# The step size dt leaves the decay exponent: masked C·B products are multiplied by it on GpSimd

## The chip, the cores and the metric

One core of a Trainium2 chip runs the whole program. The metric is the device time of one execution in microseconds (us), the median of several runs. "The profile" and "the trace" are one profiled execution of the same program. The engines are TensorE (PE, matrix products; PEld are its weight loads), VectorE (DVE), ScalarE (ACT), GpSimd (POOL) and SyncE (SP, which here only starts DMAs). Each runs its own instructions in order and waits for the others on semaphores.

## The reference

One layer over 512 latent tokens with a context prefix of 256 tokens, D = 1024, all in f32. It has a token mixer (a bidirectional Mamba-2 scan of 16 heads in 4 groups, beside a gated short convolution, one input and one output projection) and then a PEER mixer, which for every token picks 16 experts in each of 8 heads and gathers their rows. The part that this case is about is the scan inside a chunk of 128 tokens:

```python
xdt = xs * dt[..., None]                      # per token and head
acs = jnp.cumsum(a, axis=2)                   # a = dt * A, log decay
seg = acs[:, :, :, None] - acs[:, :, None, :]
decay = jnp.exp(jnp.where(lower, seg, -jnp.inf))
cb = jnp.einsum('bclgn,bcsgn->bclsg', cm, bm)
y_diag = jnp.einsum('bclsg,bclsgr,bcsgrp->bclgrp', cb, decay, xdt)
...
y_f, h_f = ssd_direction(xs, bm, cm, dt[:, :, 0], a[:, :, 0], h0_fwd, False)
y_b, h_b = ssd_direction(xs, bm, cm, dt[:, :, 1], a[:, :, 1], h0_bwd, True)
return y_f + y_b, h_f, h_b
...
y = y + d_skip * xs
```

So each pair (s, l) of tokens of a chunk has a forward factor for s <= l and a backward one for s >= l; on the diagonal both count, with decay 1 and their two step sizes dt.

## The kernel before

The 512 tokens are four tiles of 128 (m = 0 to 3), the context two more. The program has these stages, in order: set-up and the input projection for x, B and C (up to about 205 us); z, transposes and cumulated decays (to 250 us); the state-space stage (250 to 391 us), which also carries the projections of the short convolution for the first half of the tokens; the output projection, normalisation and first queries of tile 0 and in part 1 (to 465 us); and the gather, in which GpSimd starts 512 indirect DMAs of expert rows while VectorE and TensorE use them, and the second half of the mixer's work is threaded in between.

The order of the state-space stage is written out by hand in the list SCHED, and each engine walks this list and issues its own part of every entry. There are ten `step` entries (chunk states, forward and backward in turn) with the `x` entries that prepare their inputs. Then for each tile m and each group g there are `r` (select decays), `m` (the product `mdec` of decays and C·B), `y` (TensorE's diagonal product), `diag` after each second group, `off` and `out` (the part of the states that enter the chunk) and `cb` (C·B of the next tile, placed at the end of the tile before). `proj` entries, 24 in all, stand between them. This text calls a pair (m, g) block b = 4m + g.

For one block: ScalarE starts the load of two rows of cumulated decays for each of four heads, spread over all partitions, into one of three buffers `drows`, two blocks ahead (`load_rows`; it waits until `mdec` of the block before has been formed). `log_decays` (L1280, eight ACTIVATE) adds a bias per partition, `adec`, which is ln(dt) minus the cumulated decay of the row token, for both directions. VectorE's `select_decays` (L1790) picks forward or backward by a triangular mask. ScalarE takes the exponential (L1312). VectorE's `decay_matrix` (L1804) multiplies by C·B into one of three buffers `mdec`. TensorE's `diagonal` (L936) multiplies by `xs`. The selection keeps only one direction on the diagonal; the other one's share, dt times the diagonal of C·B, is added to the skip factor.

C·B itself: TensorE fills a bank (L923), ScalarE copies it to SBUF (L1304, two buffers `cbm`), and VectorE's `c_times_b` (L1777 to L1782) takes out the diagonal by a product with the identity and a sum, and makes `skip`, which `diagonal_part` (L1813) multiplies by `xs`; L1815 adds the bank of the diagonal products. `output` is L1824 (bank times decay), L1827 (add) twice per direction and L1830 (times z). The state update `step` is L1746 and L1748 for each half. L1758, L1759, L1619 are the short convolution's input product and taps, L1765 its gate. L1843 scales groups of y.

On ScalarE the squares of y (`group_squares`, L1242) of tile m − 1 stand behind block (m, 3). On GpSimd this stage has only `squares` of the short convolution (L706, L710, L713), eight times; it walks SCHED for them and holds them back until three `r` entries have gone by. ScalarE's `sc_scale` waits for them two channels later. GpSimd's earlier work, the modulation (L687 to L694), ends at 212 us.

Of the kernel before, what the change touches and what calls it, by code (L numbers as in the profile page):

```python
# [15 lines left out]
ALU = mybir.AluOpType  # L16
ACT = mybir.ActivationFunctionType
AX = mybir.AxisListType.X

P = 128  # L20
# [9 lines left out]
def build(nc, x, x_t, ctx_in, ctx_t, rows_a, rows_b, w_ada, w_in, w_dt, conv_w, dt_bias, a_log, d_skip, w_out, w_q, keys,  # L30
# [311 lines left out]
    with ExitStack() as stack:  # L342
# [3 lines left out]
        def sem(name):  # L346
            return stack.enter_context(nc.semaphore(name))
# [40 lines left out]
        mdec = [at(k, HPG * P) for k in (52, 54, 98)]  # L388
        NMD = len(mdec)
# [52 lines left out]
        cbm = [at(k, NG, P) for k in (128, 130)]  # L442
        cbd, skip = at(135, NG), at(135.25, 2, HEADS)
        cbi = at(132, NG, P)
# [29 lines left out]
        s_cbm, s_ln = sem("cb_products_copied"), sem("steps_logged")  # L474
# [182 lines left out]
        def _(pool):  # L657
# [56 lines left out]

            waiting, n_r = [], 0
            for kind, n in SCHED:
                if kind == "r":
                    n_r += 1
                    if waiting and n_r >= waiting[0][1] + 3:
                        squares(waiting.pop(0)[0])  # L720
                elif kind == "proj" and projs[n][0] == "gb":
                    waiting.append((projs[n][1], n_r))
# [41 lines left out]
        def _(pe):  # L764
# [162 lines left out]
            def diagonal(mg):  # L927
                m, g = mg
                b = m * NG + g
                name = ("y", m, g // 2)  # L930
                yps = claim(name) if g % 2 == 0 else bank_of(name)
                pe.wait_ge(s_m, b + 1)
                for r in range(HPG):
                    h = g * HPG + r
                    col = (h % 8) * HD
                    last = mm(yps[:, col:col + HD], mdec[b % NMD][:, r * P:(r + 1) * P],  # L936
                              xs[:, m, h * HD:(h + 1) * HD], start=True, stop=True)
# [205 lines left out]
        def _(act):  # L1143
# [69 lines left out]
            A(dtl, dts[:], ACT.Ln).then_inc(s_ln, 1)  # L1213
# [74 lines left out]
            for kind, n in SCHED:  # L1288
# [11 lines left out]
                elif kind == "cb":  # L1300
                    ps = await_bank(act, ("cb", n))
                    if n >= 2:
                        act.wait_ge(s_m, (n - 1) * NG)
                    ins = A(cbm[n % 2].rearrange("p g l -> p (g l)"), ps[:, :], ACT.Copy)  # L1304
                    release(ins, ("cb", n))
                    await_read(act, ("cb", n))
                    act.sem_inc(s_cbm, 1)
                elif kind == "r":
# [12 lines left out]
                    if g == NG - 1 and 1 <= m <= NA:  # L1321
                        group_squares(m - 1)
# [215 lines left out]
        def _(dve):  # L1538
# [170 lines left out]
            V.sem_inc(s_acs, 1)  # L1709
            dve.wait_ge(s_edec, 3)  # L1710
# [64 lines left out]
            def c_times_b(m):  # L1775
                dve.wait_ge(s_cbm, m + 1)
                link(V.tensor_tensor(cbi, cbm[m % 2], ident[:].unsqueeze(1).to_broadcast([P, NG, P]), ALU.mult))  # L1777
                link(V.tensor_reduce(out=cbd, in_=cbi, axis=mybir.AxisListType.X, op=ALU.add))
                s = skip[:, m % 2].rearrange("p (g r) -> p g r", r=HPG)
                link(V.tensor_tensor(s, dts[:, 0, m, :].rearrange("p (g r) -> p g r", r=HPG),  # L1780
                                     cbd.unsqueeze(2).to_broadcast([P, NG, HPG]), ALU.mult))
                link(V.tensor_tensor(skip[:, m % 2], skip[:, m % 2], drow[:], ALU.add))  # L1782
# [10 lines left out]
            def decay_matrix(mg):  # L1793
                m, g = mg
                b = m * NG + g
                if b >= NMD:
                    f = b - NMD
                    if f % 2:
                        await_filled(dve, ("y", f // NG, (f % NG) // 2))
                    else:  # L1800
                        dve.wait_ge(s_mu, f // 2 + 1)
                dve.wait_ge(s_cbm, m + 1)
                dve.wait_ge(s_dexp, b + 1)
                V.tensor_tensor(mdec[b % NMD].rearrange("p (r l) -> p r l", l=P),  # L1804
                                cbm[m % 2][:, g].unsqueeze(1).to_broadcast([P, HPG, P]),
                                drows[b % NDR][:, 0].rearrange("p (r l) -> p r l", l=P), ALU.mult).then_inc(s_m, 1)

            def diagonal_part(mh):

                m, h = mh  # L1810
                cols = slice(h * 512, (h + 1) * 512)
                y = yacc[m][:, cols]
                link(V.tensor_tensor(heads(y), heads(xs[:, m, cols]), per_head(skip[:, m % 2, 8 * h:8 * h + 8], 8), ALU.mult))  # L1813
                ps = await_bank(dve, ("y", m, h))
                read_link(V.tensor_tensor(y, y, ps[:, :], ALU.add), ("y", m, h))  # L1815
# [48 lines left out]
            for kind, n in SCHED:  # L1864
# [332 lines left out]
```

## Time and profile before

| what | value |
|---|---|
| median of 3 runs (lowest to highest) | 1859.75 us (1859.25 to 1860.06) |
| the profiled execution's own time | 1860.06 us |
| its span in the trace | 1858.2 us |
| busy: PE, DVE, ACT, POOL | 76%, 77%, 30%, 46% |
| DMA, mean over the span | 356 GB/s |
| 286 to 390 us: PE, DVE, ACT, POOL busy | 94.4, 80.2, 57.5, 11.3 us of 104 |

Times in the trace count from the start of the span. Busy time of an engine doesn't contain its waits, but a VectorE or GpSimd instruction that is held up after it started is shown longer. "L1804" is line 1804 of the kernel. A matmul in f32 shows as two instructions. "Idle before" is the time in which the engine had nothing running just before the named group, and behind the arrow is what ended it.

### The profile page before, as it was taken

To read this page: it belongs to the slowest core of one execution; us is meant where nothing else is said; L and a number is where in the kernel's file an instruction comes from. 1 tells how busy PE (TensorE), PEld (TensorE's weight loads), DVE (VectorE), ACT (ScalarE), POOL (GpSimd) and SP (SyncE) were. 2 spreads that over 40 slices of the span, in tenths; PEclk is the share of its full clock that TensorE was granted. 3 is DMA by queue.
4 is the path that set the end of the run, shared out by engine and by line. 5 is a ranking of instruction groups with operands and counts; after the bars stand their busy time and mean duration, and the time that the engine had idled before them with its cause. 6 is when DMAs were issued, how large, how long until landed. Compare 5 with 4: busy or idle time off the path is not lost.

```text
span 1858.2 us, 15417 instructions
## 1 busy us (share of the span) xinstructions
PE 1404.9 (76%) x4381; PEld 810.2 (44%) x4381; DVE 1439.6 (77%) x2790; ACT 552.4 (30%) x1566; POOL 861.9 (46%) x622
## 2 busy tenths in 40 slices
PE   7999999999688878877878777687655555565554
PEld 2555687888355545544545244343311111111111
DVE  1555468655878779889877988798989889888877
ACT  3110234622332343223313432233322223222222
POOL 0788500011545444444434465456555555555561
PEclk9999999999899999898998799788877787877777
DMA  9543325564999999999999999999999999999996
GB/s 380 193 157 136 137 92 158 165 267 178 386 411 421 421 421 421 421 421 421 420 421 421 370 416 421 422 422 421 422 421 421 422 421 422 421 421 421 422 422 249
DMA packets 95723, 660.96 MB, mean 356 GB/s; under 512 B 10766, under 2 KB 11286, under 8 KB 17302
## 3 DMA queue, kind: packets, MB, share of 16 engines
q0 software_dynamic: 76448, 555.78, 72.6%
q1 hardware_dynamic: 13808, 93.39, 12.8%
q10 hardware_dynamic: 5383, 10.80, 1.9%
q8 instruction: 36, 0.59, 0.1%
q14 instruction: 48, 0.39, 0.1%
HBM read 657.76 MB, written 2.18 MB: 355 GB/s over the span
## 4 chain that ended last, share of the span: by engine, by line
DMA 44%; PE 23%; DVE 20%; issue 6%; ACT 4%; POOL 1%; SPq 0%; DVEq 0%; ACTq 0%; POOLq 0%
DMA arena<-in_peer_uv,arena 42%; PE bank L826 10%; DVE arena L2053 7%; PE bank L1111 5%; DVE arena L2089 4%; PE bank L999 3%; DMA arena<-in_w_ada 2%; PE bank L851 1%; POOL arena L758 1%; DMA arena<-acs_scratch 1%; ACT arena L1472 1%; DVE arena L2016 1%; ACT arena L1280 1%; DVE arena L1746 1%; DVE arena L1748 1%
## 5 line engine op out<-in xcount | busy, mean ns | idle before, releaser
L758 POOL DMA_INDIRECT arena<-in_peer_uv,arena x512 | 707.8, 1382 | 721.6 <-DVE arena L2089 446.3
L1111 PE MATMUL bank<-arena,smalls 128*128 128x512 f32 x1036 | 663.0, 775 | 415.9 <-ACT smalls L1480 415.7
L2053 DVE CUSTOM_DVE_ANT_0 arena<-arena 128x1024 f32<-128x1024 f32 x512 | 619.4, 1223 | 153.3 <-DMA arena<-in_peer_uv,arena 151.8
L1111 PEld LDWEIGHTS bank<-arena,smalls 128*128 128x128 f32 x1036 | 220.2, 231 | 783.5 <-ACT smalls L1480 588.9
L2089 DVE SCALAR_TENSOR_TENSOR arena<-arena 128x1024 f32<-128x1024 f32 x247 | 315.8, 1278 | 37.4 <-ACT arena L1472 34.8
L826 PE MATMUL bank<-arena 128*128 128x256 f32 (+1 forms) x1216 | 329.0, 428 | 1.8 <-ACT arena L1176 1.5
L1467 ACT ACTIVATE arena<-arena 128x2 f32<-128x2 f32 x255 | 51.9, 203 | 925.1 <-DVE arena L2053 925.0
L826 PEld LDWEIGHTS bank<-arena 128*128 128x128 f32 x1216 | 232.7, 192 | 100.9 <-issue 76.1
L1472 ACT ACTIVATE arena<-arena 128x1 f32<-128x1 f32 x510 | 122.5, 287 | 8.5
L1054 PE MATMUL bank<-arena 128*128 128x256 f32 x480 | 108.9, 380 | 0.0
L1480 ACT ACTIVATE smalls<-ident,arena 128x128 f32<-128x128 f32 x259 | 103.6, 401 | 8.3
L1054 PEld LDWEIGHTS bank<-arena 128*128 128x128 f32 x480 | 91.2, 191 | 23.0 <-issue 12.0
L1641 DVE TENSOR_SCALAR arena<-bank,early 128x512 f32<-128x512 f32 (+1 forms) x28 | 18.4, 692 | 67.3 <-PE bank L826 67.3
L687 POOL TENSOR_TENSOR arena<-arena,cs 128x2048 f32<-128x2048 f32 x16 | 57.7, 3606 | 22.3 <-DVE arena L1629 13.5
L1619 DVE SCALAR_TENSOR_TENSOR arena<-bank,early,arena 128x496 f32<-128x496 f32 (+1 forms) x112 | 62.6, 622 | 0.6
L1032 PE MATMUL bank<-arena 128*128 128x256 f32 x256 | 59.6, 387 | 0.0
L851 PE MATMUL bank<-arena 128*128 128x256 f32 x256 | 58.1, 384 | 0.0
L1032 PEld LDWEIGHTS bank<-arena 128*128 128x128 f32 x256 | 50.2, 197 | 15.5 <-issue 9.3
L999 PE MATMUL bank<-arena 128*128 128x256 f32 x256 | 56.0, 379 | 0.0
L851 PEld LDWEIGHTS bank<-arena 128*128 128x128 f32 x256 | 49.4, 194 | 10.7 <-issue 4.4
L710 POOL TENSOR_TENSOR arena<-arena 128x256 f32<-128x256 f32 x7 | 5.4, 775 | 104.3 <-DVE arena L1765 104.3
L999 PEld LDWEIGHTS bank<-arena 128*128 128x128 f32 x256 | 48.4, 190 | 6.5
(282 smaller groups left out, 1216.3 us busy)
## 6 DMA issues: line engine op xcount, KB each, us to landing
arena<-in_w_in SPq DMA_DIRECT2D x40, 1024.0 KB, 8.3
arena<-in_w_ada POOLq DMA_DIRECT2D x16, 1024.0 KB, 5.1
arena<-in_w_out SPq DMA_DIRECT2D x16, 1024.0 KB, 9.4
arena<-in_peer_w_q SPq DMA_DIRECT2D x16, 1024.0 KB, 9.1
arena<-in_w_ada SPq DMA_DIRECT2D x8, 1024.0 KB, 12.9
arena<-acs_scratch ACTq DMA_DIRECT2D x16, 512.0 KB, 4.7
arena<-in_peer_uv,arena POOLq DMA_INDIRECT x512, 19.6
arena<-in_x SPq DMA_DIRECT2D x4, 512.0 KB, 12.2
```

Source lines behind the costliest of these rows:

```text
L758: nc.gpsimd.indirect_dma_start(gslot[slot], None, uv_tab[0], bass.IndirectOffsetOnAxis(eid[t % 2][:, k:k + 1], 0)).then_inc(s_gsl[slot], 16)
L826: last = mm(dst, w[:, k, j * P:(j + 1) * P], hT(k), start=(k == 0), stop=(k == KD - 1))
L851: last = mm(ps[:, i * WCOL:(i + 1) * WCOL], hT_tile(halves[half][i], k), w[:, k, :], start=(k == 0), stop=(k == KD - 1))
L999: last = mm(ps[:, i * WCOL:(i + 1) * WCOL], src, w[:, k, :], start=(k == 0), stop=(k == KD - 1))
L1032: last = mm(ps[:, i * WCOL:(i + 1) * WCOL], src, w[:, k, :], start=(k == 0), stop=(k == KD - 1))
L1054: last = mm(ps[:, i * WCOL:(i + 1) * WCOL], h2T[:, m % NA, k, :], w[:, k, :], start=(k == 0), stop=(k == KD - 1))
L1111: last = mm(acc[h][:, :], diag[:, k % NDG], row_v(n)[:, h * 512:(h + 1) * 512], start=first, stop=last_one)
L1472: A(wexp[:, k + i:k + i + 1], gate[t % 2][:, k + i:k + i + 1], ACT.Copy, scale=gelu[:, k + i:k + i + 1]).then_inc(s_wexp, 1)
L1480: A(diag[:, r % NDG], ident[:], ACT.Copy, scale=wexp[:, k + i:k + i + 1]).then_inc(s_diag, 1)
L1619: return V.scalar_tensor_tensor(out=d, in0=s, scalar=w, in1=d, op0=ALU.mult, op1=ALU.add)
L2053: V.tensor_tensor_reduce(row_u(n), row_u(n), h2[t], 1.0, 0.0, ALU.mult, ALU.add, dots[:, k:k + 1]).then_inc(s_dot, 1)
L2089: V.scalar_tensor_tensor(out=vacc, in0=row_v(n), scalar=w, in1=vacc, op0=ALU.mult, op1=ALU.add).then_inc(s_vadd, 1)
```

## The change

- The logarithm of dt on ScalarE and the operation that forms `adec` from it go. `adec` is now minus the cumulated decay, made earlier, right behind the cumulated sums.
- ScalarE's copy of C·B goes. VectorE reads the bank and writes C·B times the upper and times the lower triangle mask into SBUF (`cbm[:, 0]` and `cbm[:, 1]`, one buffer for the tile), both with the diagonal. `skip` goes, and `diagonal_part` uses the plain skip factor `drow`.
- GpSimd gets `dt_times_cb` at each `r`: two products with dt per head, one for each direction, and their sum, into one of two buffers `mdec`. For this it waits until the diagonal product of two blocks before has been done, and at g = 0 for the masked products.
- VectorE's `decay_matrix` waits for GpSimd and multiplies `mdec` by the decays in place.
- ScalarE's squares of y move from g = 3 to g = 1.

```diff
-        mdec = [at(k, HPG * P) for k in (52, 54, 98)]
-        NMD = len(mdec)
+        mdec = at(52, 2, HPG * P)
+        mback = at(96, 2, HPG * P)
...
+            def dt_times_cb(mg):
+
+                m, g = mg
+                b = m * NG + g
+                if b == 0:
+                    await_filled(pool, ("st", len(steps) - 2, 1))
+                if b >= 2:
+                    f = b - 2
+                    if f % 2:
+                        await_filled(pool, ("y", f // NG, (f % NG) // 2))
+                    else:
+                        pool.wait_ge(s_mu, f // 2 + 1)
+                if g == 0:
+                    pool.wait_ge(s_cbm, m + 1)
+                hs = slice(g * HPG, (g + 1) * HPG)
+                dst = [v[:, b % 2].rearrange("p (r l) -> p r l", l=P) for v in (mdec, mback)]
+                for d in range(2):
+                    nc.gpsimd.tensor_tensor(dst[d], cbm[:, d, g].unsqueeze(1).to_broadcast([P, HPG, P]),
+                                            dts[:, d, m, hs].unsqueeze(2).to_broadcast([P, HPG, P]),
+                                            ALU.mult).then_inc(s_dtcb, 1)
+                pool.wait_ge(s_dtcb, 3 * b + 2)
+                nc.gpsimd.tensor_tensor(mdec[:, b % 2], mdec[:, b % 2], mback[:, b % 2], ALU.add).then_inc(s_dtcb, 1)
...
                 if kind == "r":
+                    dt_times_cb(n)
...
-            A(dtl, dts[:], ACT.Ln).then_inc(s_ln, 1)
...
-                elif kind == "cb":
-                    ps = await_bank(act, ("cb", n))
-                    if n >= 2:
-                        act.wait_ge(s_m, (n - 1) * NG)
-                    ins = A(cbm[n % 2].rearrange("p g l -> p (g l)"), ps[:, :], ACT.Copy)
-                    release(ins, ("cb", n))
-                    await_read(act, ("cb", n))
-                    act.sem_inc(s_cbm, 1)
...
-                    if g == NG - 1 and 1 <= m <= NA:
+                    if g == 1 and 1 <= m <= NA:
                         group_squares(m - 1)
...
+            V.tensor_scalar(adec[:], acs[:], -1.0, None, ALU.mult).then_inc(s_neg, 1)
...
             def c_times_b(m):
-                dve.wait_ge(s_cbm, m + 1)
-                link(V.tensor_tensor(cbi, cbm[m % 2], ident[:].unsqueeze(1).to_broadcast([P, NG, P]), ALU.mult))
-                link(V.tensor_reduce(out=cbd, in_=cbi, axis=mybir.AxisListType.X, op=ALU.add))
...
+                cb = await_bank(dve, ("cb", m)).rearrange("p (g l) -> p g l", g=NG)
+                tri_g = lambda tri: tri[:].unsqueeze(1).to_broadcast([P, NG, P])
+                post(V.tensor_tensor(cbm[:, 0], cb, tri_g(upper), ALU.mult))
+                read_link(V.tensor_tensor(cbm[:, 1], cb, tri_g(lower), ALU.mult), ("cb", m))
+                V.sem_inc(s_cbm, 1)
...
-                dve.wait_ge(s_cbm, m + 1)
+                dve.wait_ge(s_dtcb, 3 * (b + 1))
                 dve.wait_ge(s_dexp, b + 1)
-                V.tensor_tensor(mdec[b % NMD].rearrange("p (r l) -> p r l", l=P),
-                                cbm[m % 2][:, g].unsqueeze(1).to_broadcast([P, HPG, P]),
-                                drows[b % NDR][:, 0].rearrange("p (r l) -> p r l", l=P), ALU.mult).then_inc(s_m, 1)
+                V.tensor_tensor(mdec[:, b % 2], mdec[:, b % 2], drows[b % NDR][:, 0], ALU.mult).then_inc(s_m, 1)
...
-                elif kind == "step" and n == 0:
-                    dve.wait_ge(s_ln, 1)
-                    V.tensor_tensor(adec[:], dtl, acs[:], ALU.subtract).then_inc(s_neg, 1)
-                    step(0)
```

## Rows read from the trace of the kernel before

**Rows 1.** The page, span in 40 slices: busy tenths of the DMA engines.
```profile
DMA  9543325564999999999999999999999999999996
```

**Rows 2.** Stretches of 20 us: busy time of each engine, granted TensorE clock, DMA.
```profile
280.00:300.00 20.00, 15.47 (x70) 12.61 (x69) 17.28 (x29) 8.43 (x22) 1.67 (x2) 0.91 0.50 155
300.00:320.00 20.00, 20.00 (x109) 17.86 (x108) 16.84 (x29) 10.47 (x30) 1.72 (x2) 1.00 0.47 135
```

**Rows 3.** Groups by line, 250 to 392 us: busy, mean ns | idle before, releaser.
```profile
L936 PE MATMUL bank<-arena 128*128 128x64 f32 x128 | 16.9, 275 | 9.6 <-DVE arena L1804 9.5
L1790 DVE COPY_PREDICATED arena<-early,arena 128x512 f32<-128x512 uint32 x16 | 11.8, 740 | 8.7 <-ACT arena L1280 8.4
L1804 DVE TENSOR_TENSOR arena<-arena 128x512 f32<-128x512 f32 x16 | 11.3, 706 | 4.6 <-ACT arena L1312 4.3
L1815 DVE TENSOR_TENSOR arena<-arena,bank 128x512 f32<-128x512 f32 x8 | 5.5, 687 | 0.6 <-PE bank L936 0.3
L1304 ACT ACTIVATE arena<-bank 128x512 f32<-128x512 f32 x4 | 2.3, 587 | 9.1 <-PE bank L923 9.1
```

**Rows 4.** The chain that ended last, 320 to 350 us: start, us, what.
```profile
324.25 8.82 DMA arena<-acs_scratch
```

**Rows 5.** Timeline of TensorE, 290 to 395 us: start, us, what [idle before].
```profile
290.00 1.09 PE L936 MATMUL bank<-arena 128*128 128x64 f32 x8 [2.50 <-DVE arena L1804]
290.92 5.36 PE L826 MATMUL bank<-arena 128*128 128x256 f32 x16
297.90 1.10 PE L936 MATMUL bank<-arena 128*128 128x64 f32 x8 [1.62 <-DVE arena L1804]
298.84 3.67 PE L826 MATMUL bank<-arena 128*128 128x256 f32 x16
...
389.30 1.10 PE L936 MATMUL bank<-arena 128*128 128x64 f32 x8
...
394.57 13.98 PE L999 MATMUL bank<-arena 128*128 128x256 f32 x64
```

**Rows 6.** Three lines of GpSimd's modulation: ns min/median/max, first and last start.
```profile
L687 POOL TENSOR_TENSOR arena<-arena,cs x16: 3592/3614/3617, 53.1 to 204.2; 128x2048 f32<-128x2048 f32 x16
...
L690 POOL TENSOR_TENSOR arena<-arena x16: 2341/2348/2357, 56.8 to 207.9; 128x1024 f32<-128x1024 f32 x16
...
L692 POOL TENSOR_TENSOR arena<-arena x16: 1261/1267/1275, 59.2 to 210.3; 128x512 f32<-128x512 f32 x16
```

**Rows 7.** Timeline of all engines, 272.2 to 274.4 and 324.2 to 327.
```profile
272.30 1.22 DVE L1726 TENSOR_TENSOR arena<-arena,smalls 128x1024 f32<-128x1024 f32 x1
272.46 1.53 POOL L706 TENSOR_TENSOR arena<-arena 128x256 f32<-128x256 f32 x1 [60.09 <-DVE arena L1765]
273.44 1.10 DVE L1746 TENSOR_TENSOR arena<-arena,smalls 128x512 f32<-128x512 f32 x1
...
325.00 0.74 DVE L1804 TENSOR_TENSOR arena<-arena 128x512 f32<-128x512 f32 x1 [0.50 <-ACT arena L1312]
325.27 1.05 POOL L713 TENSOR_TENSOR arena<-arena 128x256 f32<-128x256 f32 x1
325.67 1.21 DVE L1813 TENSOR_TENSOR arena<-arena 128x512 f32<-128x512 f32 x1
```

**Rows 8.** Timeline of VectorE, 286 to 369 us.
```profile
286.67 0.73 DVE L1790 COPY_PREDICATED arena<-early,arena 128x512 f32<-128x512 uint32 x1
...
309.54 0.69 DVE L1777 TENSOR_TENSOR arena<-arena,ident 128x512 f32<-128x512 f32 x1 [0.90 <-ACTq L1307]
...
311.41 0.73 DVE L1790 COPY_PREDICATED arena<-early,arena 128x512 f32<-128x512 uint32 x1
...
319.68 0.74 DVE L1790 COPY_PREDICATED arena<-early,arena 128x512 f32<-128x512 uint32 x1
...
337.76 0.69 DVE L1777 TENSOR_TENSOR arena<-arena,ident 128x512 f32<-128x512 f32 x1 [2.20 <-ACTq L1307]
...
366.67 0.69 DVE L1777 TENSOR_TENSOR arena<-arena,ident 128x512 f32<-128x512 f32 x1 [4.02 <-ACTq L1307]
```

More of the change, by code:

```diff
@@ L441, in build @@
         yacc = [at(160, D)] * NA + [yB[:, m] for m in range(NA)]
-        cbm = [at(k, NG, P) for k in (128, 130)]
-        cbd, skip = at(135, NG), at(135.25, 2, HEADS)
-        cbi = at(132, NG, P)
+        cbm = at(128, 2, NG, P)
         iota_j, iota_i = sb("iota_j", [P, TOP]), sb("iota_i", [P, TOP], mybir.dt.int32)
@@ L473, in build @@
         s_neg, s_ldec = sem("decay_sums_negated"), sem("log_decays_formed")
-        s_cbm, s_ln = sem("cb_products_copied"), sem("steps_logged")
+        s_cbm, s_dtcb = sem("masked_products_ready"), sem("dt_times_products_step")
         s_ldsel, s_dexp = sem("log_decays_selected"), sem("decays_formed")
@@ L935, in diagonal @@
                     col = (h % 8) * HD
-                    last = mm(yps[:, col:col + HD], mdec[b % NMD][:, r * P:(r + 1) * P],
+                    last = mm(yps[:, col:col + HD], mdec[:, b % 2, r * P:(r + 1) * P],
                               xs[:, m, h * HD:(h + 1) * HD], start=True, stop=True)
@@ L1775, in c_times_b @@
             def c_times_b(m):
-                dve.wait_ge(s_cbm, m + 1)
-                link(V.tensor_tensor(cbi, cbm[m % 2], ident[:].unsqueeze(1).to_broadcast([P, NG, P]), ALU.mult))
-                link(V.tensor_reduce(out=cbd, in_=cbi, axis=mybir.AxisListType.X, op=ALU.add))
[L1779 to L1782, printed above, removed]
+                cb = await_bank(dve, ("cb", m)).rearrange("p (g l) -> p g l", g=NG)
[3 more added lines that the diff above has]
+                V.sem_inc(s_cbm, 1)
             def select_decays(mg):
@@ L1795, in decay_matrix @@
                 b = m * NG + g
[L1796 to L1801, printed above, removed]
-                dve.wait_ge(s_cbm, m + 1)
+                dve.wait_ge(s_dtcb, 3 * (b + 1))
                 dve.wait_ge(s_dexp, b + 1)
-                V.tensor_tensor(mdec[b % NMD].rearrange("p (r l) -> p r l", l=P),
-                                cbm[m % 2][:, g].unsqueeze(1).to_broadcast([P, HPG, P]),
-                                drows[b % NDR][:, 0].rearrange("p (r l) -> p r l", l=P), ALU.mult).then_inc(s_m, 1)
+                V.tensor_tensor(mdec[:, b % 2], mdec[:, b % 2], drows[b % NDR][:, 0], ALU.mult).then_inc(s_m, 1)
             def diagonal_part(mh):
@@ L1812, in diagonal_part @@
                 y = yacc[m][:, cols]
-                link(V.tensor_tensor(heads(y), heads(xs[:, m, cols]), per_head(skip[:, m % 2, 8 * h:8 * h + 8], 8), ALU.mult))
+                link(V.tensor_tensor(heads(y), heads(xs[:, m, cols]), per_head(drow[:, 8 * h:8 * h + 8], 8), ALU.mult))
                 ps = await_bank(dve, ("y", m, h))
```

## The prediction

> **What bounds the kernel now.** I read the page first, then stretches, groups and single instructions of the one stage that the diff touches. The DMA line of the page [rows 1] shows two halves: up to slice 10 the DMA engines are partly idle, from about 465 us on they are at 9 tenths in every slice but the last. That second half is the gather of expert rows. Nothing in the diff enters it, so what the first half gains or loses moves the end by about the same amount. The diff lies at 250 to 391 us, in the state-space stage, whose last diagonal product is on TensorE at 389.30 and whose output weights follow at 394.57 [rows 5].
>
> Call the 16 pairs (tile m, group g) blocks b = 4m + g. TensorE can't start a block's diagonal product before VectorE has written `mdec` (L1804). The groups of 250 to 392 us [rows 3] show TensorE idle 9.6 us in front of those products, 9.5 of it for L1804, which is all that its 94.4 busy us leave free of the 104 from 286 to 390. So the stage is bound by two engines in turn: TensorE's own work, plus 9.6 us in which VectorE is late. VectorE is late at b = 0 and 1 (products at 290.00 and 297.90, idle 2.50 and 1.62 before them [rows 5]), and again from b = 9 on. At 324.25 the chain of work passes through the load of a block's decay rows, 8.82 us [rows 4]. At the start of each tile VectorE waits for ScalarE's copy of the C·B product: 0.90, 2.20 and 4.02 us for m = 1, 2, 3 [rows 8].
>
> **The change part by part.**
>
> *ScalarE.* The four copies of C·B (0.587 us each, L1304 [rows 3]) go, and so does the logarithm of dt. VectorE can read the bank as soon as TensorE has filled it. The move of the four squares from g = 3 to g = 1 takes them from in front of that copy. Its new place costs nothing: they stand where ScalarE waits for the next selection.
>
> *VectorE, C·B.* The product with the identity, the reduction and two small operations, 1.87 us with their gaps from 309.54 to 311.41 [rows 8], are replaced by two mask products that read a bank. The nearest row is L1815, also 128x512 with one input in a bank: 0.687 us [rows 3]. That is 1.43 us with gaps, 0.44 less per tile. With the wait the gains at the start of the tiles are up to 1.3, 2.6 and 4.4 us for m = 1, 2, 3.
>
> *GpSimd.* It now forms C·B·dt: for every block two products and, after a wait for both, a sum, all 128x512. The sum has an exact row, L692: 1.27 us [rows 6]. The products have a broadcast operand and have none at this size. L687 (broadcast, 2048 columns) is 3.61 us. L690 and L692 (1024 and 512 columns, 2.35 and 1.27) leave a fixed part of 2 x 1.27 − 2.35 = 0.19 us; with it L687's slope gives 0.19 + 3.42 / 4 = 1.04 us for 512 columns. The ends are 0.90 (a quarter of L687) and L692's 1.27. I take 1.04, since L687 is the one row with a broadcast. A block is then 1.04 + 1.04 + 1.27 + three gaps of 0.08 = 3.6 us, 4.05 at the other end, and 16 blocks are 58 to 65 us on an engine that had 11.3 us of work from 286 to 390. In the Trainium skill, "GPSIMD Engine Reference", section "Performance versus the Vector engine", a two-input addition over 2048 columns is 4497 ns; by that rate a product would be an estimated 1.12 us and the block 3.8 us. L687's 3.61 us for as many columns is below it.
>
> *The new wait.* VectorE's L1804 waits for GpSimd's third operation of the block; queued behind it are the state updates and outputs, the next selection (L1790) and, through it, ScalarE's exponential, its load of decay rows and TensorE.
>
> *The collisions.* While GpSimd multiplies two tiles, a VectorE operation with two inputs in SBUF doesn't run beside it. Three of them are in the trace [rows 7]. L1746 is 1.10 us at 273.44, against 0.69, which an operation of this size takes alone (L1777, [rows 8]), and GpSimd's first product, asked for at 272.46 during a 1.22 us VectorE operation, took 1.53 us. At 325.27 GpSimd's sum took 1.05 us, as VectorE's L1804 was on; then VectorE's L1813 took 1.21 us instead of 0.69. Each waits for the end of the other's operation, less about 0.1 us, and they alternate. The selection, L1804, L1813, L1827, L1830, the convolution taps and L1746 have two SBUF inputs; L1824, L1815, L1748 and the new mask products read a bank and have one. The skill says the same in "SBUF — State Buffer", section "Who interferes with whom": the one that comes second blocks until the first has finished. If the two merely shared the bandwidth the sum below would be nearer to rival 1.
>
> **The sum, replayed.** I follow the milestones with the durations above, and alternation wherever both want SBUF.
> 1. GpSimd's first squares now stand behind three blocks, which takes the collision of 273.44 away: −0.4. With −0.4 for C·B of m = 0, the masked products are ready 0.8 us before 286.67 (the selection's start [rows 8]), at 285.85.
> 2. GpSimd's three operations collide with the selection and a tap and end at 290.5; the start of block 1 then holds VectorE once more. `mdec` of b = 0 comes at 292.15 instead of 289.85: +2.3.
> 3. Eight state operations (8 x 0.72 = 5.8 us) stand before the next selection, four of them (L1746) with two SBUF inputs. Alternating with GpSimd's blocks 1 and 2 they cost four times 0.4 us: b = 1 comes at +4.0, and TensorE's product 297.90 at 301.9. From there to b = 8 it has no gap to give back [rows 2].
> 4. m = 1: the masked products gain 1.2, leaving +2.8. Until the selection of b = 5 (319.68 [rows 8]) VectorE has two outputs of four operations, L1804 and L1830, GpSimd has blocks 4 and 5. Alternation costs 0.3 + 0.4 + 0.9 + 0.4 + 0.4 + 0.6, about 2.9: +5.7, and b = 5 comes at +6.
> 5. b = 6, 7: TensorE is dense and keeps the +6.
> 6. m = 2: the copy's wait is gone (2.20 and 0.43), but the selection now waits for its row load, issued 5 to 6 us later and landing after 8.8 us: +3. With 2 of contention the next selection is at +5.
> 7. m = 3: of 4.4 us that can be gained all but 0.6 of the +5 is; contention again costs 2.9: +3.6. Taps and the group scaling (two more operations with two SBUF inputs) add 1.4. The product of 389.30 comes at about 394.3: +5.
>
> The profiled execution was 1860.06 us with a span of 1858.2, and the median of the runs 1859.75. +5 on the median gives **1864.8 us**, 0.27% slower. A difference under about 0.2% (3.7 us) can't be told from no change.
>
> **The rivals.**
> *Rival 1, the losses stay in the gaps.* Half the contention (GpSimd's blocks mostly run while VectorE waits or reads banks). For it: VectorE is idle for a quarter of the stage; from 300 to 320 us TensorE is busy without a gap [rows 2], so a late `mdec` can be hidden there. Then b = 1 is +2.5, tile 1 +2.8, the waits recovered at m = 2 and 3 take it to between −1 and +3: 1859 to 1863 us, within 0.2%. Against it: both engines are started by the same event, the end of the mask products, so they collide by construction.
> *Rival 2, faster.* The mechanism is that ScalarE's copy and the squares in front of it leave the start of m = 2 and m = 3. Without any contention the replay gives b = 1 at +0.35, the selections of m = 2 and 3 at −2.6 and −7, and TensorE's own work as the floor: the last product at 383.6, −5.7 us, 1854 us. It decides from the point at which collisions cost under 1.5 us a tile. Against it the 1.21 and 1.10 us rows.
> *Rival 3, GpSimd is the bound.* Products at 1.27 us and each operation held 0.4 us make a block 5.3 us, 16 blocks 84 us, the seven squares some 12 more, and waits for two buffers instead of three: it fills the 104 us. Then TensorE waits before nearly every block, +9 to +12: about 1870 us.
> *TensorE's clock.* In 280 to 300 us it was granted 0.91, elsewhere in the stage 1.00 [rows 2]: after the gap of 2.50 us the 16 products at 290.92 took 5.36 us instead of 3.67 (that stretch was in part at 1.2 GHz, the others at 2.4), while gaps of 1.6 us had no such effect. The gaps before b = 0 and b = 1 become 4.7 and 3.4 us. A second slow stretch, behind b = 1, would go straight on to the end: +1.7. It is an upper bound inside the forecast, as the first slow stretch is hidden by the wait for b = 1.
>
> **How the numbers follow.** Forecast (alternation, +3.5 to +7.5): 0.48. Rival 1: 0.32. Rival 2: 0.08. Rival 3: 0.12. The forecast lies above 3.7 us nearly whole, rival 3 whole: slower 0.58; rival 1 and a rest of the forecast: same 0.34; faster 0.08. The range leaves out rival 2 and the upper half of rival 3: 1858 to 1870 us.
>
> **What would show it.** In the profile after: GpSimd's products at about 1.04 us alone and longer beside VectorE; L1790, L1804, L1746 and L1827 with means above 0.69 to 0.74 us; TensorE idle before its diagonal products well over 9.6 us, most of it at b = 0 and 1 (301.9 for the second); the mask products of m = 1, 2 and 3 starting at once when TensorE's C·B ends; output weights at about 399.6 instead of 394.57; the gather unchanged but later. The prediction is wrong if those means stay where they are, if GpSimd's blocks are much shorter than 3.6 us, or if the end doesn't follow the stage's end.

## The result, and the profile after

The changed kernel took 1875.7 us (median of 4 runs, 1874.26 to 1876.53), the kernel before 1859.5 us beside it (4 runs). The ratio is 1.0087 with a 95% interval of 1.0069 to 1.0104: 0.87% slower, 16.2 us. Forecast were 1864.8 us and a range up to 1870. The direction was right, the size a third of the true one, and the time lies outside the range.

The span grew from 1858.2 to 1873.9 us, by 15.7. All of it is there at the end of the state-space stage. TensorE's timeline of the changed kernel (start, us, what, idle before), to be laid beside [rows 5]:

```profile
292.16 1.94 PE L958 MATMUL bank<-arena 128*128 128x64 f32 x8 [4.66 <-DVE arena L1810]
293.89 4.90 PE L848 MATMUL bank<-arena 128*128 128x256 f32 x16
301.27 1.10 PE L958 MATMUL bank<-arena 128*128 128x64 f32 x8 [2.47 <-DVE arena L1810]
...
323.85 1.00 PE L958 MATMUL bank<-arena 128*128 128x64 f32 x8
...
331.76 1.97 PE L958 MATMUL bank<-arena 128*128 128x64 f32 x8 [3.41 <-DVE arena L1810]
333.52 5.56 PE L848 MATMUL bank<-arena 128*128 128x256 f32 x16
338.92 1.00 PE L958 MATMUL bank<-arena 128*128 128x64 f32 x8
...
362.92 1.10 PE L958 MATMUL bank<-arena 128*128 128x64 f32 x8 [2.99 <-DVE arena L1810]
363.86 5.36 PE L848 MATMUL bank<-arena 128*128 128x256 f32 x16
...
404.89 1.10 PE L958 MATMUL bank<-arena 128*128 128x64 f32 x8 [0.28 <-DVE arena L1810]
...
410.17 13.98 PE L1021 MATMUL bank<-arena 128*128 128x256 f32 x64
```

L958 is the diagonal product (L936 before). Block 0 starts 2.2 us later than before, block 1 3.4, block 15 15.6 (404.89 against 389.30) and the output weights 15.6 (410.17 against 394.57). From there the two traces are the same, only shifted. The same 80 us, counted from nearly the same place (first the kernel before, then the changed one; busy time of PE, PEld, DVE, ACT, POOL, clock, DMA):

```profile
390.00:470.00 80.00, 76.81 (x369) 66.13 (x369) 39.49 (x112) 18.50 (x42) 11.99 (x12) 1.00 0.60 235
```

```profile
406.00:486.00 80.00, 76.81 (x366) 65.66 (x365) 39.24 (x110) 18.52 (x42) 11.93 (x12) 1.00 0.60 235
```

So the loss is made between 286 and 405 us. The groups of the changed kernel from 250 to 410 us, by shape (busy us, mean ns | idle before):

```profile
L848 PE MATMUL bank<-arena 128*128 128x256 f32 x374 | 89.6, 396 | 0.0
L730 POOL TENSOR_TENSOR arena<-arena,smalls 128x512 f32<-128x512 f32 x32 | 44.1, 1398 | 106.9 <-DVEq L1794 99.1 <-PE bank L958 7.6
L734 POOL TENSOR_TENSOR arena<-arena 128x512 f32<-128x512 f32 x16 | 24.6, 1536 | 1.3
L958 PE MATMUL bank<-arena 128*128 128x64 f32 x128 | 18.6, 293 | 20.2 <-DVE arena L1810 20.2
L1802 DVE COPY_PREDICATED arena<-early,arena 128x512 f32<-128x512 uint32 x16 | 16.1, 1006 | 5.1 <-ACT arena L1301 4.3
L1810 DVE TENSOR_TENSOR arena<-arena 128x512 f32<-128x512 f32 x16 | 15.3, 955 | 10.7 <-ACT arena L1325 6.9 <-POOL arena L734 3.6
L1632 DVE SCALAR_TENSOR_TENSOR arena<-arena,early 128x252 f32<-128x252 f32 x16 | 12.9, 808 | 0.6
L1831 DVE TENSOR_TENSOR arena<-arena 128x512 f32<-128x512 f32 x13 | 10.8, 833 | 0.4
L1828 DVE TENSOR_TENSOR arena<-bank,smalls 128x512 f32<-128x512 f32 x14 | 9.6, 686 | 0.2
L1773 DVE TENSOR_SCALAR arena<-arena,early 128x256 f32<-128x256 f32 x8 | 3.8, 476 | 0.3
L1792 DVE TENSOR_TENSOR arena<-bank,early 128x512 f32<-128x512 f32 x4 | 2.8, 692 | 0.6 <-PE bank L945 0.5
```

TensorE's idle time before its diagonal products is 20.2 us, against 9.6 [rows 3]. That is 10.6 us of the 15.6. The other 5 us are products at the lower clock: the 16 projection products that took 3.67 us at 2.4 GHz took 4.90, 5.56 and 5.36 us behind three gaps (before: one such stretch, 5.36), and two diagonal products 1.94 and 1.97 instead of 1.10. This divides TensorE's time; what of the 5 us is on the path is a question for the runs below.

The reason for the idle time is in VectorE's means. The selection (L1802) rose from 0.740 to 1.006 us and the decay product (L1810) from 0.706 to 0.955 [rows 3]. The taps (L1632) are at 0.808, the adds of the outputs (L1831) at 0.833. In the kernel before, 250 to 392 us, these two and the TENSOR_SCALAR in front of the taps were:

```profile
L1827 DVE TENSOR_TENSOR arena<-arena 128x512 f32<-128x512 f32 x12 | 8.3, 692 | 0.4
L1619 DVE SCALAR_TENSOR_TENSOR arena<-arena,early 128x252 f32<-128x252 f32 x16 | 7.7, 481 | 0.6
L1759 DVE TENSOR_SCALAR arena<-arena,early 128x256 f32<-128x256 f32 x8 | 2.8, 353 | 0.3
```

The operations that read a bank aren't longer: L1828 takes 0.686 us (L1824 before: 0.685), and the mask products L1792, which are new, take 0.692. The first four groups alone hold VectorE for (16.1 − 11.8) + (15.3 − 11.3) + 16 x (0.808 − 0.481) + 13 x (0.833 − 0.692) = 15.3 us more. VectorE waits for GpSimd's sum only 3.6 us (in front of L1810).

One such place, block 5 of the changed kernel, with GpSimd at its block 6 (timeline of all engines):

```profile
324.63 1.22 DVE L1834 TENSOR_TENSOR arena<-arena 128x1024 f32<-128x1024 f32 x1
324.93 3.28 POOL L730 TENSOR_TENSOR arena<-arena,smalls 128x512 f32<-128x512 f32 x2 [0.89 <-PE bank L958]
...
325.88 1.47 DVE L1802 COPY_PREDICATED arena<-early,arena 128x512 f32<-128x512 uint32 x1
327.24 0.40 DVE L1772 TENSOR_TENSOR arena<-arena,bank 128x256 f32<-128x256 f32 x1
...
328.29 1.27 POOL L734 TENSOR_TENSOR arena<-arena 128x512 f32<-128x512 f32 x1
...
328.39 2.19 DVE L1632 SCALAR_TENSOR_TENSOR arena<-arena,early 128x252 f32<-128x252 f32 x2
...
330.61 1.10 DVE L1810 TENSOR_TENSOR arena<-arena 128x512 f32<-128x512 f32 x1
```

GpSimd asks for its first product at 324.93, is let in when L1834's reading ends, and from then on each side waits for the other: the selection takes 1.47 us instead of 0.74, two taps 2.19 instead of 1.00, the decay product 1.10 instead of 0.69. TensorE sits idle for 3.41 us until the last of them (331.76). The 0.40 us operation that reads a bank goes through.

### The profile page after: what moved, and what is told of

The parts are those of the page before. It is cut to its first block, busy times and chain, and to the rows that moved or that the text cites. A ratio compares the mean times of both kernels' runs of the same rounds, so it can differ in the third digit from the quotient of the medians.

```text
span 1873.9 us, 15441 instructions
## 1 busy us (share of the span) xinstructions
PE 1419.2 (76%) x4381; PEld 818.5 (44%) x4381; DVE 1456.2 (78%) x2782; ACT 547.2 (29%) x1559; POOL 924.3 (49%) x670
## 4 chain that ended last, share of the span: by engine, by line
DMA 42%; PE 23%; DVE 22%; issue 6%; ACT 4%; POOL 2%; SPq 0%; DVEq 0%; POOLq 0%; ACTq 0%
DMA arena<-in_peer_uv,arena 41%; PE bank L848 10%; DVE arena L2053 7%; PE bank L1133 5%; DVE arena L2089 4%; PE bank L1021 3%; DMA arena<-in_w_ada 2%; PE bank L873 1%; POOL arena L780 1%; DVE arena L1632 1%; ACT arena L1485 1%; DVE arena L2016 1%; DVE arena L1760 1%; ACT smalls L1493 1%; DVE arena L1762 1%
## 5 line engine op out<-in xcount | busy, mean ns | idle before, releaser
L1133 PE MATMUL bank<-arena,smalls 128*128 128x512 f32 x1036 | 670.2, 783 | 406.1 <-ACT smalls L1493 404.6
L730 POOL TENSOR_TENSOR arena<-arena,smalls 128x512 f32<-128x512 f32 x32 | 44.1, 1398 | 106.9 <-DVEq L1794 99.1
L1632 DVE SCALAR_TENSOR_TENSOR arena<-bank,early,arena 128x496 f32<-128x496 f32 (+1 forms) x112 | 62.6, 621 | 0.6
L1054 PEld LDWEIGHTS bank<-arena 128*128 128x128 f32 x256 | 50.4, 197 | 15.6 <-issue 9.2
## 6 DMA issues: line engine op xcount, KB each, us to landing
arena<-in_x SPq DMA_DIRECT2D x4, 512.0 KB, 12.3
```

Of the source, the lines that this page charges most:

```text
L1054: last = mm(ps[:, i * WCOL:(i + 1) * WCOL], src, w[:, k, :], start=(k == 0), stop=(k == KD - 1))
L1133: last = mm(acc[h][:, :], diag[:, k % NDG], row_v(n)[:, h * 512:(h + 1) * 512], start=first, stop=last_one)
L1632: return V.scalar_tensor_tensor(out=d, in0=s, scalar=w, in1=d, op0=ALU.mult, op1=ALU.add)
```

## The experiments

Two theories stood against each other. **Collisions**: VectorE's operations with two SBUF inputs and GpSimd's reads hold each other up. **The wait**: VectorE's decay product comes late because GpSimd's block takes 4 us. All ratios are to the kernel before on the same chip, with 95% intervals. The stage begins up to 2.5 us earlier or later from one profiled execution to the next. Where two traces are compared, the last diagonal product is therefore counted from VectorE's copy of the cumulated sums, at 247.31 us in the kernel before and at 247.74 in the changed one: 142.0 us before, 157.2 changed. These counts vary as well, by some 3 us between executions of kernels that take the same time: with the squares early alone, a run below, it is 139.2 us.

**The change without GpSimd's part.** dt is left out of the diagonal products, and the diagonal's backward share too.

```diff
                 if kind == "r":
-                    dt_times_cb(n)
...
-                dve.wait_ge(s_dtcb, 3 * (b + 1))
...
-                V.tensor_tensor(mdec[:, b % 2], mdec[:, b % 2], drows[b % NDR][:, 0], ALU.mult).then_inc(s_m, 1)
+                V.tensor_tensor(mdec[:, b % 2].rearrange("p (r l) -> p r l", l=P),
+                                cbm[:, 0, g].unsqueeze(1).to_broadcast([P, HPG, P]),
+                                drows[b % NDR][:, 0].rearrange("p (r l) -> p r l", l=P), ALU.mult).then_inc(s_m, 1)
```

> The changed kernel without GpSimd's three operations: VectorE multiplies the forward masked product by the decays, so dt is left out of the diagonal products and the diagonal's backward share too. Everything else of the change stays. Both theories (the new wait on GpSimd, and the collisions of GpSimd with VectorE) say that the whole loss is GpSimd's: the stage then ends 2 to 6 us before that of the kernel before, 1854 to 1858 us, and TensorE's idle time before its diagonal products falls from 20.2 to under 8 us. The rival, that the loss comes from other parts of the change (the mask products on VectorE, the moved squares, two buffers), says 1865 us or more.

Measured: 0.9977 (0.9964 to 0.9990), 1856.9 us. All the rest of the change together is a gain of 0.23%. TensorE is idle 6.0 us before its diagonal products, and the last of them comes 137.1 us after the cumulated sums (382.81 and 245.76), 4.9 earlier than before. The whole loss comes with GpSimd's part.

**Collisions without the wait.** The kernel before, with GpSimd's three operations added for every block. `extra` waits as `dt_times_cb` does and forms the identity times dt twice and a sum of the result with itself, of the same size; nobody reads what it writes.

```diff
                 if kind == "r":
+                    extra(n)
```

> The kernel before, with three GpSimd operations of the same size and operands' forms at every block (identity times dt twice, and a sum), started under the same waits, into a place that nobody reads. Collisions without the wait. If the collisions are the cause: VectorE's selection and decay product have means of 0.95 to 1.0 us as in the changed kernel, TensorE is idle 17 us or more before its products, 1868 to 1874 us. If the wait is the cause: within 3 us of the kernel before, 1859 to 1863 us. Between the two if they share it: 1864 to 1867.

Measured: 1.0083 (1.0064 to 1.0101), 1877.9 us. Work that nobody waits for costs as much as the change. Its groups, 250 to 410 us:

```profile
L732 POOL TENSOR_TENSOR arena<-ident,smalls 128x512 f32<-128x512 f32 x32 | 41.8, 1305 | 114.8 <-PE bank L941 69.4 <-ACTq L1332 24.7 <-PE bank L961 19.2
L1815 DVE COPY_PREDICATED arena<-early,arena 128x512 f32<-128x512 uint32 x16 | 20.0, 1248 | 5.4 <-ACT arena L1305 5.1
L961 PE MATMUL bank<-arena 128*128 128x64 f32 x128 | 19.4, 302 | 17.8 <-DVE arena L1829 17.8
```

The selection is at 1.248 us here, though nothing on VectorE waits for the added operations. The last product comes 158.9 us after the sums (408.68 and 249.77).

**The wait without collisions.** The changed kernel, with fills of constants in place of GpSimd's products and sum; VectorE then multiplies the decays by 1, so C·B and dt are left out.

```diff
                 for d in range(2):
-                    nc.gpsimd.tensor_tensor(dst[d], cbm[:, d, g].unsqueeze(1).to_broadcast([P, HPG, P]),
...
-                nc.gpsimd.tensor_tensor(mdec[:, b % 2], mdec[:, b % 2], mback[:, b % 2], ALU.add).then_inc(s_dtcb, 1)
+                    nc.gpsimd.memset(at(96, 2 * HPG * P), 1.0).then_inc(s_dtcb, 1)
...
+                nc.gpsimd.memset(at(96, 2 * HPG * P), 1.0).then_inc(s_dtcb, 1)
...
+                nc.gpsimd.memset(mdec[:, b % 2], 1.0).then_inc(s_dtcb, 1)
```

> The changed kernel with GpSimd's three operations replaced by four fills of constants that take about as long in all (3 of 1024 columns and 1 of 512, some 3.7 us by the 0.204 us of 128 columns) and read no SBUF; what VectorE multiplies is then 1 instead of C·B times dt. The wait without the collisions of reads. If the wait is the cause: 1868 to 1876 us with VectorE's operations back at 0.69 to 0.74 us. If the collisions are: 1856 to 1862 us.

Measured: 0.9970 (0.9958 to 0.9983), 1854.9 us, as fast as without GpSimd's part. The last product comes 136.7 us after the sums (382.89 and 246.23), 5.3 earlier than before.

```profile
L728 POOL MEMSET arena<- 128x1024 f32 x32 | 30.5, 954 | 103.1 <-DVEq L1792 95.2 <-PE bank L956 7.0
L956 PE MATMUL bank<-arena 128*128 128x64 f32 x128 | 16.5, 272 | 5.6 <-DVE arena L1808 5.6
L1800 DVE COPY_PREDICATED arena<-early,arena 128x512 f32<-128x512 uint32 x16 | 12.5, 781 | 8.8 <-ACT arena L1299 8.1
L1808 DVE TENSOR_TENSOR arena<-arena 128x512 f32<-128x512 f32 x16 | 11.6, 725 | 5.7 <-ACT arena L1323 4.5 <-POOL arena L732 1.1
L732 POOL MEMSET arena<- 128x512 f32 x16 | 8.4, 525 | 0.9
L1771 DVE TENSOR_SCALAR arena<-arena,early 128x256 f32<-128x256 f32 x8 | 4.3, 536 | 0.3
```

A block's three long fills and one short one take 3 x 0.95 + 0.53 = 3.4 us on GpSimd. In the changed kernel two products and a sum take as long when nothing disturbs them (2 x 1.04 + 1.27, the shortest of each), and 4.3 us on average (44.1 + 24.6 for 16 blocks), as VectorE holds them up. The waits are the same, and VectorE's selection is at 0.781 us. A wait for a block of 3.4 us costs nothing that the stage's end shows; what costs is that GpSimd reads. VectorE waits 1.1 us here for GpSimd's last fill, against 3.6 for the sum in the changed kernel: this longer wait comes from the collisions too, but no run has it alone.

**A third of GpSimd's reading.** The changed kernel with the forward product alone; the backward product and the sum are left out.

```diff
-                for d in range(2):
+                for d in range(1):
...
-                pool.wait_ge(s_dtcb, 3 * b + 2)
-                nc.gpsimd.tensor_tensor(mdec[:, b % 2], mdec[:, b % 2], mback[:, b % 2], ALU.add).then_inc(s_dtcb, 1)
```

> The changed kernel with one of GpSimd's three operations per block, the forward product; the backward product and the sum are left out. If the loss grows with the time in which GpSimd reads SBUF: a third of the way from the run with writes alone (0.30% faster than the kernel before) to the changed kernel (0.87% slower), so 0 to 0.2% slower, 1860 to 1864 us. If it has a threshold, because a short GpSimd operation fits into VectorE's pauses: 0.1 to 0.3% faster, 1855 to 1858 us.

Measured: 0.9991 (0.9981 to 1.0001), 1858.5 us, between the two forecasts. GpSimd's product is at 1.269 us, VectorE's selection at 0.809. From writes only to one reading operation the ratio grows by 0.0021, from one to three by 0.0096, where a straight line would give 0.0042. That fits first collisions that fall partly into VectorE's pauses; the three runs don't show more than that the cost grows faster than the reading.

**The squares back at g = 3**, in the changed kernel.

```diff
-                    if g == 1 and 1 <= m <= NA:
+                    if g == NG - 1 and 1 <= m <= NA:
```

> The changed kernel with the squares of y back at g = 3. Neither theory gives their place a role, as ScalarE's copy is gone: within 2 us of the changed kernel, 1874 to 1878 us. The rival, that in their new place they delay ScalarE's exponentials, says 1869 to 1873 us.

Measured: 1.0083 (1.0066 to 1.0102), the changed kernel's time. **The squares early, alone**, in the kernel before (the reverse edit):

> The kernel before, with ScalarE's squares of y moved from g = 3 to g = 1, alone. In the kernel before they stand in front of the copy of C·B, 1.6 us each for m = 2 and 3, at places where TensorE is later late. If that wait is on the path: 1.5 to 3 us faster than the kernel before. If it is hidden behind the load of the decay rows and TensorE's own work: within 1 us.

Measured: 0.9999 (0.9991 to 1.0008). Their place makes no difference in either kernel. In the trace of the second the last product comes 139.2 us after the sums (384.85 and 245.70).

**Three buffers** in the changed kernel, in free SBUF.

```diff
-        mdec = at(52, 2, HPG * P)
-        mback = at(96, 2, HPG * P)
+        mdec = [at(k, HPG * P) for k in (52, 54, 132)]
+        mback = [at(k, HPG * P) for k in (96, 98, 134)]
```

> The changed kernel with three buffers instead of two for GpSimd's products, so that GpSimd may be one more block ahead. GpSimd waited 7.6 us in all for TensorE's products. If GpSimd's lateness counts: 3 us or more faster than the changed kernel. As the run with writes alone showed no cost of the wait, and more work ahead only moves the collisions: within 2 us of the changed kernel, either way.

Measured: 1.0094 (1.0080 to 1.0108). GpSimd no longer waits for TensorE, and nothing is gained.

**TensorE's clock.** The changed kernel, with unused products in front of the waits for the late blocks, so that TensorE isn't idle. First 64 columns wide.

```diff
+FILL = {0: 16, 1: 8, 5: 12, 9: 10}
...
+                for n in range(FILL.get(b, 0)):
...
+                    mm(yps[:, col:col + HD], ident[:], xs[...], start=True, stop=True)
                 pe.wait_ge(s_m, b + 1)
```

> The changed kernel, with products that nobody uses on TensorE in front of the waits for the blocks 0, 1, 5 and 9 (16, 8, 12 and 10 products of 64 columns, into the bank that the true products then overwrite), so that it isn't idle there. In the changed kernel three stretches behind such gaps ran in part at 1.2 GHz, 4.9, 5.6 and 5.4 us where 3.7 is usual. If these stretches are part of the path: 3 to 5 us faster than the changed kernel, so 10 to 13 us over the kernel before. If VectorE's lateness alone sets it: within 1 us of the changed kernel, 15 to 17 over.

Measured: 1.0082 (1.0069 to 1.0095), and there are still four slow stretches, behind the blocks 0, 5, 10 and 13. The one behind block 9 is gone. TensorE's timeline at block 0:

```profile
285.76 3.68 PE L958 MATMUL bank<-arena,ident 128*128 128x64 f32 x32
290.49 1.97 PE L964 MATMUL bank<-arena 128*128 128x64 f32 x8 [1.05 <-DVE arena L1816]
292.25 6.17 PE L849 MATMUL bank<-arena 128*128 128x256 f32 x16
```

Then as wide as the projections' products:

```diff
+FILL = {0: 10, 1: 5, 3: 2, 5: 7, 9: 6, 10: 2, 13: 4, 14: 4}
...
+                half = (g % 2) * GW
+                for n in range(FILL.get(b, 0)):
+                    mm(yps[:, half:half + GW], ident[:], xs[...], start=True, stop=True)
```

> The changed kernel with unused products of 256 columns, as wide as the projections' products that ran at 2.4 GHz, on TensorE in front of the waits for the blocks 0, 1, 3, 5, 9, 10, 13 and 14; those of 64 columns took no slow stretch away. If the slow stretches come from what TensorE does in its gaps: none or one is left of the stretches of 5.4 us, and if they are on the path, 3 to 5 us less than the changed kernel, 0.6 to 0.7% over the kernel before. If VectorE's lateness alone sets the end: the same time as the changed kernel within 0.1%, 0.8 to 0.95% over.

Measured: 1.0076 (1.0059 to 1.0093). Of the slow stretches one is left, behind block 1; the groups of 250 to 410 us and TensorE's timeline:

```profile
L849 PE MATMUL bank<-arena 128*128 128x256 f32 x375 | 86.7, 386 | 0.0
L962 PE MATMUL bank<-arena 128*128 128x64 f32 x128 | 16.9, 275 | 6.2 <-DVE arena L1814 6.2
```

```profile
287.47 4.48 PE L957 MATMUL bank<-arena,ident 128*128 128x256 f32 x20
292.20 1.10 PE L962 MATMUL bank<-arena 128*128 128x64 f32 x8 [0.25 <-DVE arena L1814]
...
302.39 5.30 PE L849 MATMUL bank<-arena 128*128 128x256 f32 x16
...
403.21 1.10 PE L962 MATMUL bank<-arena 128*128 128x64 f32 x8 [0.36 <-DVE arena L1814]
```

TensorE got back 89.6 + 18.6 − 86.7 − 16.9 = 4.6 us of its own time, and the last product came only 1.8 us earlier (155.4 us after the sums, 403.21 and 247.85, against 157.2). Both were run once more on one chip:

> The changed kernel once more, beside the next run on the same chip, so that the two can be compared: 0.8 to 0.95% slower than the kernel before.

> The changed kernel with the wide unused products once more, on the same chip as the run above. The first time only one slow stretch was left and the last diagonal product came 1.7 us earlier than in the changed kernel. If the slow clock has that share, the ratio is 0.1% lower than that of the run above; if the 4.9 us that the slow stretches take of TensorE's time are all on the path, 0.25% lower; if none is, the same within 0.03%.

Measured: 1.0076 (1.0064 to 1.0088) for the changed kernel, 1.0070 (1.0057 to 1.0083) with the wide products. They differ by 0.0006, and each interval reaches 0.0012 or more to either side, so the times don't settle the share. The traces say more. The changed kernel with the squares back at g = 3 had no slow stretch behind block 5, after the same gap:

```profile
332.15 1.10 PE L958 MATMUL bank<-arena 128*128 128x64 f32 x8 [3.40 <-DVE arena L1810]
333.09 3.67 PE L848 MATMUL bank<-arena 128*128 128x256 f32 x16
```

Starts of three diagonal products, in us after the cumulated sums:

| run | 16 products behind block 5 | block 5 | block 8 | block 15 |
|---|---|---|---|---|
| changed kernel | 5.56 | 84.0 | 107.7 | 157.2 |
| changed kernel, again | 5.07 | 84.0 | 106.7 | 156.1 |
| squares back at g = 3 | 3.67 | 84.1 | 105.0 | 154.6 |
| wide unused products | 3.67 | 85.0 | 105.9 | 155.4 |
| wide unused products, again | 3.67 | 84.9 | 105.9 | 157.0 |

A slow stretch behind block 5 costs up to 2.7 us, and the end keeps them: from block 8 to block 15 all but the last row take some 49.5 us. In the last row a slow stretch of 5.36 us behind block 10 adds 1.7. The one behind block 9 costs nothing: block 10 comes 7.3 us after block 9 with it (changed kernel) and without it (wide products), as TensorE then waits longer for VectorE. The wide products have a price of their own, which hid the gain: those in front of block 3 made it 0.9 us late. So the slow clock is 0 to 2.7 us of the loss, another amount in another execution.

**A version without GpSimd's part.** The kernel before, where VectorE reads C·B's bank itself, with the squares at g = 1.

```diff
-                dve.wait_ge(s_cbm, m + 1)
-                link(V.tensor_tensor(cbi, cbm[m % 2], ident[:].unsqueeze(1).to_broadcast([P, NG, P]), ALU.mult))
+                cb = await_bank(dve, ("cb", m)).rearrange("p (g l) -> p g l", g=NG)
+                post(V.tensor_tensor(cbi, cb, ident[:].unsqueeze(1).to_broadcast([P, NG, P]), ALU.mult))
+                read_link(V.tensor_copy(cbm[m % 2], cb), ("cb", m))
+                V.sem_inc(s_cbm, 1)
```

> The kernel before, with the squares at g = 1 and with VectorE reading C·B's bank itself: it multiplies the bank by the identity and copies it to SBUF, and ScalarE's copy goes. GpSimd gets nothing, ln(dt) stays in the exponent. One operation of 0.7 us more on VectorE per tile, against waits of 0.9, 2.2 and 4.0 us. By the run without dt, which was 0.23% faster, 2 to 4 us faster than the kernel before. If VectorE's extra operation costs what the wait gave: within 1 us.

Measured: 0.9982 (0.9971 to 0.9992), 1857.5 us: 0.18% faster than the kernel before. It keeps most of what the run without dt gained, and computes everything.

## Why the prediction failed in size

The mechanism was right: the loss is GpSimd's, it is made by collisions in SBUF, the rest of the change is a small gain, and the stage's end moves the kernel's end one to one. Two runs isolate it: 0.83% slower for collisions alone, 0.30% faster for the wait alone. The Trainium skill ("SBUF — State Buffer", section "Who interferes with whom") has that mechanism, down to the difference that the run with fills shows: two SBUF inputs against a GpSimd operation that reads, not against one that only writes. One part isn't separated: GpSimd's part costs 1.10% in the changed kernel (1.0087 against 0.9977 without it), the unused operations cost 0.83%. The difference is about as wide as the intervals; it may be the 3.6 us for which VectorE waits for GpSimd's slowed sum, or nothing.

The step that failed is the price of the collisions in the replay (steps 3 to 7), and with it the slow clock behind block 5, which step 5 put at nothing. By the steps, how many us later than in the kernel before (forecast, then measured):

| step | place | forecast | measured |
|---|---|---|---|
| 2 | product of block 0 | +2.3 | +2.2 |
| 3 | product of block 1 | +4.0 | +3.4 |
| 3 | product of block 3 | +4.0 | +4.9 |
| 4 | selection of block 4, start | +2.8 | +3.8 |
| 4 | selection of block 5, end | +5.7 | +6.9 |
| 4 | product of block 5 | +6 | +8.5 |
| 5 | product of block 7 | +6 | +11.3 |
| 6 | selection of block 8, start | +3 | +8.7 |
| 6 | selection of block 9, end | +5 | +12.8 |
| 6 | product of block 12 | +5 | +13.8 |
| 7 | selection of block 12, start | +0.6 | +9.6 |
| 7 | selection of block 13, end | +3.6 | +12.3 |
| 7 | product of block 15 | +5 | +15.6 |

The selections at the start of the tiles, m = 1, 2 and 3 in the changed kernel, then m = 2 and 3 in the kernel before (m = 1 is in [rows 8]):

```profile
315.19 0.75 DVE L1802 COPY_PREDICATED arena<-early,arena 128x512 f32<-128x512 uint32 x1
...
348.30 0.73 DVE L1802 COPY_PREDICATED arena<-early,arena 128x512 f32<-128x512 uint32 x1
...
378.18 0.75 DVE L1802 COPY_PREDICATED arena<-early,arena 128x512 f32<-128x512 uint32 x1
```

```profile
339.62 0.73 DVE L1790 COPY_PREDICATED arena<-early,arena 128x512 f32<-128x512 uint32 x1
...
368.54 0.73 DVE L1790 COPY_PREDICATED arena<-early,arena 128x512 f32<-128x512 uint32 x1
```

Added up, the forecast has losses of 2.3 + 1.7 + 2.9 + 0.3 + 2 + 2.9 + 1.4 = 13.5 us and returns at the starts of the tiles, where waits become shorter than before, of 1.2 + 3 + 4.4 = 8.6. The trace has returns of 1.1 + 2.6 + 4.2 = 7.9, nearly as forecast, and losses of 23.5. Of the 10 us of loss that the forecast lacks 2.8 are the clock in this execution, and the rest arose where VectorE works beside GpSimd:

- *GpSimd's product* was rightly put at 1.04 us: the shortest take 1.04. On average they take 1.40, and the block 4.3 us and not 3.6, because each waits for VectorE.
- *Step 3* had nothing more behind block 1. By block 3 another 1.5 us were lost: beside GpSimd's block 3 the selection of block 2 took 1.30 us and `diagonal_part` 1.76.
- *Step 4*, the contention of a tile, +2.9 up to the selection of block 5, was nearly right for what it counted: 3.1. It didn't count the taps behind it. The replay had GpSimd at blocks 4 and 5 there, and block 6 has to wait for block 4's product. But that product had been done at 324.85, before VectorE came to the selection and the taps. The taps went from 0.481 to 0.808 us each, 5.2 us over the stage, where step 7 had 1.4 for taps and group scaling together.
- *Step 5* was "TensorE is dense and keeps the +6". Block 6 lost another 2.8 us, as block 5's product and the stretch behind it, after a gap of 3.41 us, ran in part at 1.2 GHz (0.83 was granted from 320 to 340 us). The clock was priced at one more slow stretch of 1.7 us behind block 1. That one had none (3.67 us at 302.21), and blocks 5 and 9 had one each, of which the one behind block 9 cost nothing.
- *Step 6* had 3 us coming back at m = 2, and 2.6 did: the mask products began at 346.86 without a wait, and the selection was at +8.7 where TensorE was at +11.3. But then the tile's contention took 4.1 where 2 was forecast (the selection of block 9 took 1.45 us, the product with z in front of it 2.17 instead of 1.23, and VectorE waited 1.2 for GpSimd's sum), and blocks 10 to 12 lost 1.1 more.
- *Step 7* had 4.4 us coming back at m = 3, and 4.2 did. The contention up to the selection of block 13 was 2.7 (forecast 2.9). The operations behind it (the taps, the decay product, the group scaling and the next selection) took 3.3, where 1.4 was forecast for taps and group scaling.
- *Rival 1* (collisions hidden in the gaps) is refuted by the unused operations, 0.83% slower than the kernel before. *Rival 2* named the floor rightly: −5.7 us without contention, where the run with the wait alone has its last product at −5.3. *Rival 3* (GpSimd is the bound) gave the nearest time, +9 to +12, by another mechanism: three buffers would have helped, and did not.

What would have come nearer: VectorE was busy 80.2 us of 104 in the table of before. The replay added contention only where two chains of operations were laid side by side by hand. Take an allowance over the whole stage instead. GpSimd reads for 16 x 3.35 = 54 us of 104. Some 75 operations of VectorE with two SBUF inputs then meet it about every second time, and wait about 0.5 us ([rows 7]: 1.21 instead of 0.69). That is an estimate of 20 us of losses; VectorE's busy time between 286 us and the last product did grow by 16.9 (80.2 to 97.1). With the returns of 8.6 it gives about +11, nearer to the 15.6 than +5 is, though still short of it.

## What to carry to other kernels

Before elementwise work is moved to GpSimd, count how many of VectorE's operations beside it have two SBUF inputs: the two engines then take turns. Here 54 us of reading by GpSimd made VectorE busy for 17 us more and the kernel 16 us slower, and an unused piece of GpSimd work cost as much as the useful one. A VectorE that is busy for three quarters of a stage has little room for that, although GpSimd looks idle. When such a change is replayed, price the collision of every operation in the stage, and not only of those where the two chains are seen to meet: the waits that were to come back did come back, and the losses between them were 1.7 times the forecast.

## What the runs showed of the hardware

- VectorE's TENSOR_SCALAR of 256 columns, with one input in SBUF and its output there, also took longer: 0.353 us in the kernel before, 0.476 on average in the changed kernel, and 0.536 in the run with fills, which read nothing.
- A GpSimd operation that stands right behind the one that VectorE waits for gets in first. The decay product of block 4, released by GpSimd's sum, took 1.46 us at 320.01, as GpSimd's next product had begun at 319.89.
- After the same gap of 3.4 us in front of block 5, the product and the 16 products behind it ran in part at 1.2 GHz in the changed kernel (5.56 us, and 5.07 when run again) and wholly at 2.4 GHz with the squares back (3.67). One execution doesn't tell whether a stretch is slow.
- With unused products of 64 columns in front of block 0 and a gap of 1.05 us, that block's product and the stretch behind it were still slow (1.97 and 6.17 us), in the one execution traced; with 256 columns in the same place they were not (1.10 and 3.67), in two.
